# Two transformer blocks on one core: high-part weight tiles streamed as two 256-column products into one accumulator

## The reference, cut to what matters

```python
z = rms_norm(h) @ w_in                      # 2048 -> 5120, first block
h = h + mixed @ w_out                       # 2048 -> 2048
h = h + (silu(f @ ffn_w1) * (f @ ffn_w3)) @ ffn_w2     # 2048 -> 5632 -> 2048
h = h + (p @ pl_w_up) * sigmoid(h @ pl_w_gate)
...
proj = hn @ w_in_2                          # 2048 -> 12288, second block
y_a = pool(u) @ pool_w_2 ; y_b = (...) @ conv_out_w_2
h = h + (g_a * y_a + g_b * y_b) @ w_o_2
h = h + (silu(gate) * up) @ w_down_2        # 2048 -> 5632 -> 2048
```

## Time and profile before

| | |
|---|---|
| Device time, median of 3 runs | 2670.52 us (2670.02 to 2670.8) |
| Profiled execution, span from its first to its last instruction | 2668.2 us |
| Instructions in the profile | 39872, of them 15711 matmuls |
| DMA | 502.92 MB, mean 188 GB/s |

### The profile page before, as it was taken

How to read it: one execution, slowest core, us unless ns; L and a number is a source line. 1 busy time by engine, 2 the same in 40 slices (tenths; PEclk the granted TensorE clock), 3 DMA queues, 4 the chain that set the end, 5 groups by cost and what they waited for, 6 DMA issues and landing times.

```text
span 2668.2 us, 39872 instructions
## 1 busy us (share of the span) xinstructions
PE 2657.2 (100%) x15711; PEld 2349.5 (88%) x15711; DVE 1658.2 (62%) x1645; ACT 1235.8 (46%) x1355; POOL 0.8 (0%) x7
## 2 busy tenths in 40 slices
PE   9999999999999999999999999999999999999998
PEld 7889888888888888888999999888888888888887
DVE  6567766555655556796676666556765645564555
ACT  5446554444444444565443333444554434443444
POOL 0000000000000000000000000000000000000000
PEclk9999999999999999999999999999999999999999
DMA  8554555556555555555555555555565555555554
GB/s 291 183 174 144 192 187 189 191 189 191 192 191 191 191 191 188 175 197 198 176 183 178 179 184 190 189 189 189 189 205 189 189 190 189 189 195 195 178 190 140
DMA packets 254251, 502.92 MB, mean 188 GB/s; under 512 B 8130, under 2 KB 11652, under 8 KB 253988
## 3 DMA queue, kind: packets, MB, share of 16 engines
q1 hardware_dynamic: 252180, 497.61, 56.5%
q10 hardware_dynamic: 1952, 3.68, 0.4%
HBM read 498.37 MB, written 2.88 MB: 188 GB/s over the span
## 4 chain that ended last, share of the span: by engine, by line
PE 99%; DVE 0%; ACT 0%; DMA 0%; issue 0%; ACTq 0%; DVEq 0%
PE ps L1356 49%; PE ps L1370 24%; PE ps L1389 4%; PE ps L1390 4%; PE ps L1391 4%; PE ps L1407 4%; PE ps L1408 4%; PE ps L1409 4%; PE ps L1399 0%; PE ps L1401 0%; PE ps L1400 0%; PE ps L1319 0%; DMA xtok<-in_x_dram 0%; PE ps L1543 0%; PE ps L1542 0%; PE ps L1544 0%
## 5 line engine op out<-in xcount | busy, mean ns | idle before, releaser
L822 DVE TENSOR_TENSOR lo<-raw,hi 128x1024 fp32r<-128x1024 f32 x940 | 1127.6, 1223 | 856.5 <-ACT hi L488 847.6
L488 ACT ACTIVATE hi<-raw 128x1024 fp32r<-128x1024 f32 x940 | 971.3, 1055 | 1065.3 <-PE ps L1370 479.0
L1356 PE MATMUL ps<-A,hi 128*128 128x512 f32 x3648 | 859.9, 392 | 0.0
L1356 PEld LDWEIGHTS ps<-A,hi 128*128 128x128 f32 x3648 | 675.1, 188 | 138.9
L1356 PE MATMUL ps<-B,hi 128*128 128x512 f32 x1984 | 481.7, 395 | 0.0
L1370 PEld LDWEIGHTS ps<-A,lo 128*128 128x128 f32 x3648 | 442.6, 188 | 11.5 <-DVE lo L822 0.2
L1370 PE MATMUL ps<-A,lo 128*128 128x256 f32 x3648 | 445.4, 278 | 0.0
L1356 PEld LDWEIGHTS ps<-B,hi 128*128 128x128 f32 x1984 | 364.4, 188 | 79.3
L1370 PEld LDWEIGHTS ps<-B,lo 128*128 128x128 f32 x1984 | 243.0, 188 | 10.3
L1370 PE MATMUL ps<-B,lo 128*128 128x256 f32 x1984 | 244.5, 277 | 0.0
L1408 PE MATMUL ps<-B,hi 128*128 128x258 f32 (+1 forms) x768 | 219.8, 286 | 0.0
(11 more groups left out here) (240 smaller groups left out, 1341.1 us busy)
## 6 DMA issues: line engine op xcount, KB each, us to landing
raw<-in_w_in_dram SPq DMA_DIRECT2D x136, 1024.0 KB, 5.1
raw<-in_ffn_w_dram SPq DMA_DIRECT2D x132, 1024.0 KB, 5.1
raw<-in_w_gate_up_dram SPq DMA_DIRECT2D x88, 1024.0 KB, 5.0
raw<-in_w_down_dram SPq DMA_DIRECT2D x44, 1024.0 KB, 5.1
raw<-in_w_out_dram SPq DMA_DIRECT2D x16, 1024.0 KB, 5.1
raw<-in_pl_w_gate_dram SPq DMA_DIRECT2D x16, 1024.0 KB, 5.1
raw<-in_conv_out_w_dram SPq DMA_DIRECT2D x16, 1024.0 KB, 5.1
raw<-in_w_o_dram SPq DMA_DIRECT2D x16, 1024.0 KB, 5.1
```

The costliest lines, as they stand in the source:

```text
L488: act.activation(hi[:, slot % RING], raw[:, raw_slot, 2 * (slot % 2):2 * (slot % 2) + 2, :], ACT.Copy).then_inc(hi_ready, 1)
L822: dve.tensor_tensor(lo[:, slot % RING], raw[:, slot // 2 % RAWS, 2 * (slot % 2):2 * (slot % 2) + 2, :], hi[:, slot % RING], ALU.subtract). ...
L1356: last = pe.matmul(ps[:, b0 + m, :], high(slot, kk, m), both, start=j == 0 and kk == 0, stop=ends and j == seg.pieces - 1 and kk == 1)
```

## The change

Every product of a high weight tile with 512 columns becomes two products with 256 columns: four tiles with Xh, then the same four with Xl. All three kinds of product add to columns 0 to 255 of a bank. ACT's copy of the second accumulators and DVE's addition are taken out. DVE's first operation of each group now reads PSUM itself and frees the banks; for plup and plgate it is a plain copy. ACT waits for `psum_free` of the group where it waited for DVE's `asked`. Ahead of the first attention scores TensorE waits for `psum_free` of the last qk group. Matmuls in other layouts, loads and splits stay.

```diff
-            def copy_second(kind, G, end, b0):
-
-                act.wait_ge(pieces_used, end)
-                act.wait_ge(psum_free, G)
-                if SQUARED & {kind, before[0]}:
-                    wait(ready)
-                before[0] = kind
-                act.activation(pb_copy[:, :, :], ps[:, b0:b0 + 4, T:2 * T], ACT.Copy).then_inc(copied, 1)
+            def wait_group(G):
+
+
+                act.wait_ge(psum_free, G + 1)
+                act.nop(nofuse=True)
...
-            def add_halves(G, b0, to):
-                second.skip()
-                wait(second)
+            def sums_done(end):
+
+                dve.wait_ge(pieces_used, end)
                 wait(given)
                 wait(ready)
-                dve.tensor_tensor(to, ps[:, b0:b0 + 4, 0:T], pb_copy[:, :, :], ALU.add).then_inc(psum_free, 1)
+
+            def free_sums(ins, G):
+
+                ins.then_inc(psum_free, 1)
                 dve.wait_ge(psum_free, G + 1)
...
                 elif kind in ("gate", "ga", "gbr"):
-                    add_halves(G, b0, work[:, :, :])
-                    hand(dve.tensor_tensor(work[:, :, :], work[:, :, :], Rm, ALU.mult))
+                    sums_done(end)
+                    free_sums(dve.tensor_tensor(work[:, :, :], sums, Rm, ALU.mult), G)
...
                 elif kind in ("up", "cb"):
-                    add_halves(G, b0, work[:, :, :])
-                    step(dve.tensor_tensor(work[:, :, :], work[:, :, :], Rm, ALU.mult))
+                    sums_done(end)
+                    free_sums(dve.tensor_tensor(work[:, :, :], sums, Rm, ALU.mult), G)
...
                 elif kind == "plgate":
                     hk = some(h, k, 4, 0, T)
-                    add_halves(G, b0, work[:, :, :])
+                    sums_done(end)
+                    free_sums(dve.tensor_copy(work[:, :, :], sums), G)
...
                 X = activations(buf, layout)
+                at = 0 if layout == "halves" else META
                 pe.wait_ge(hi_ready, n + 1)
                 for kk in range(2):
                     k = 2 * j + kk + (4 * WIDEST_FIRST[g] if seg.name == "pool" else 0)
-                    for m in range(MT):
-                        both = X[:, k, 0:2 * T] if layout == "halves" else X[:, k, META:META + 2 * T]
-                        last = pe.matmul(ps[:, b0 + m, :], high(slot, kk, m), both, start=j == 0 and kk == 0,
-                                         stop=ends and j == seg.pieces - 1 and kk == 1)
+                    for part in range(2):
+                        x = X[:, k, at + part * T:at + (part + 1) * T]
+                        for m in range(MT):
+                            last = pe.matmul(ps[:, b0 + m, 0:T], high(slot, kk, m), x, start=j == 0 and kk == 0 and part == 0,
+                                             stop=ends and j == seg.pieces - 1 and kk == 1 and part == 1)
...
                         if hd == 0:
-                            v_in.skip(4)
                             wait(v_in)
+                            pe.wait_ge(psum_free, QK.g0 + 4)
```

More of the change, by code:

```diff
@@ L131 @@
 PER = {
[L132 to L135, removed]
+    "res_ffn": (2, 0, 2, 1), "part": (0, 0, 0, 0), "gate": (0, 0, 1, 0), "up": (0, 1, 1, 1),
+    "plgate": (5, 2, 4, 1), "ga": (0, 0, 1, 0), "gbr": (0, 0, 1, 0), "cv": (1, 0, 0, 0),
+    "cg": (5, 0, 0, 0), "cb": (0, 1, 1, 1), "cout": (0, 1, 1, 1), "res_ffn2": (3, 0, 2, 1),
+    "tpart": (0, 0, 0, 0),
 }
@@ L190, in turns_of @@
 def turns_of(eng, seg, tallies, run, lead=0):
-    per = [sum(PER.get(kind, (0,) * 5)[i] for kind in seg.kinds) for i in range(5)]
+    per = [sum(PER.get(kind, (0,) * 4)[i] for kind in seg.kinds) for i in range(4)]
     whole = seg.turns if seg.turns == 1 else min(seg.turns, max(seg.peel, lead))
@@ L388, in bass_two_blocks @@
         PLUP = next(s for s in SEGS if s.name == "plup")
+        QK = next(s for s in SEGS if s.name == "qk")
         def landed(n):
@@ L553, in evacuate @@
                     return
[L554 to L557, removed]
+                if kind in ("qk", "plup", "pool"):
+                    return
+                more()
+                if kind == "part":
                     return
                 if kind in ("res_ffn", "res_ffn2"):
-                    asked.skip()
-                    wait_alone(asked)
+                    wait(ready)
+                    wait_group(G)
                     given.mark(act.activation(pb_copy[:, :, :], some(h, k, 4, 0, T), ACT.Square))
@@ L579, in evacuate @@
                 elif kind == "plgate":
-                    act.wait_ge(psum_free, G + 1)
+                    wait(ready)
+                    wait_group(G)
                     given.mark(with_function(pb_copy[:, :, :], work[:, :, :], ACT.Sigmoid))
@@ L889, in evacuate @@
                     hk = some(h, k, 4, 0, T)
-                    add_halves(G, b0, work[:, :, :])
-                    step(dve.tensor_tensor(hk, hk, work[:, :, :], ALU.add))
+                    sums_done(end)
+                    free_sums(dve.tensor_tensor(hk, hk, sums, ALU.add), G)
                     more()
                 elif kind == "res_gate":
-                    add_halves(G, b0, work[:, :, :])
+                    hk = some(h, k, 4, 0, T)
+                    sums_done(end)
+                    free_sums(dve.tensor_tensor(hk, hk, sums, ALU.add), G)
                     if gi < MT - 1:
@@ L915, in evacuate @@
                 elif kind == "cout":
-                    add_halves(G, b0, work[:, :, :])
-                    step(dve.tensor_tensor(work[:, :, :], work[:, :, :], some(G2, k, 4, 0, T), ALU.mult))
+                    sums_done(end)
+                    free_sums(dve.tensor_tensor(work[:, :, :], sums, some(G2, k, 4, 0, T), ALU.mult), G)
                     hand(dve.tensor_tensor(work[:, :, :], work[:, :, :], some(G1, k, 4, 0, T), ALU.add))
@@ L921, in evacuate @@
                 elif kind == "plup":
-                    add_halves(G, b0, UP[:, k:k + 4, :])
+                    sums_done(end)
+                    free_sums(dve.tensor_copy(UP[:, k:k + 4, :], sums), G)
                 elif kind == "plgate":
                     hk = some(h, k, 4, 0, T)
-                    add_halves(G, b0, work[:, :, :])
+                    sums_done(end)
+                    free_sums(dve.tensor_copy(work[:, :, :], sums), G)
                     more()
@@ L965, in evacuate @@
                 elif kind == "pool":
-                    add_halves(G, b0, work[:, :, :])
+                    sums_done(end)
                     for i in range(MT):
-                        last = dve.scalar_tensor_tensor(out=G1[:, k + i, :], in0=work[:, i, :], scalar=gain("pscale", k + i),
+                        last = dve.scalar_tensor_tensor(out=G1[:, k + i, :], in0=ps[:, b0 + i, 0:T], scalar=gain("pscale", k + i),
                                                         in1=G1[:, k + i, :], op0=ALU.mult, op1=ALU.mult)
-                    step(last)
+                    free_sums(last, G)
                 elif kind in ("cv", "cg"):
@@ L1296, in last @@
                         dve.tensor_scalar(HT[:, a, c:e], HT[:, a, c:e], r, None, ALU.mult).then_inc(left_scaled, 1)
-            walk(dve, {0: own, 1: asked, 2: given, 3: ready, 4: second}, split, evacuate, side, last)
+            walk(dve, {0: own, 1: asked, 2: given, 3: ready}, split, evacuate, side, last)
         @block.tensor
```

28 lines of the change are left out of this document (11 added, 17 removed).

## The result

| | before | after |
|---|---|---|
| Median | 2670.44 us (2670.02 to 2670.8, 4 runs) | 2696.68 us (2690.86 to 2697.37, 4 runs) |
| Profiled execution, span | 2668.2 us | 2695.6 us |

The ratio is 1.0094, with a 95% interval of 1.0082 to 1.0106: slower, by 26.2 us. The forecast was 2686.4 us, with 2639 to 2714 as its range. The execution profiled is the longest of the four, 2697.37 us.

The account below looks back on a forecast made before the run. TensorE's distance between product starts was taken as the bound: 1299.4 us (A, PT) plus 675.0 (B) is 1974.4 against 1958.5, +15.9. With 2668.2 and 2.3 for the median that gave 2686.4 us, range 2639 to 2714.

Parts of the forecast that it names:

- What bounds the kernel: Whole span: TensorE's distance between product starts sets the time; its waits come to only 2.7 us.
- Copies, additions, waits at 0 us: ACT's copies, DVE's additions and the new waits: none ends or adds a wait of TensorE, 0 us.
- A at 117.7 ns a product: Segments reading A and PT: 3680 triples at the slow speed, 353.1 ns each, 1299.4 us.
- B at 113.4 ns: Segments reading B: 1984 triples at the fast speed, 340.2 ns each, 675.0 us.
- The prediction's own sign of being wrong: Profile after: wrong if the A stretch takes 174.2 us or B's 90.5, or TensorE waits at group starts.
- Rival 1: B keeps the slow speed it enters with from A, so everything is slow: +43.2, 2713.7 us; chance 0.25.
- stands once: 256-column runs in B: nearly all fast, one slow at 118.1 ns just after an entry from A.
- the forecast's own 2675 to 2697: Whole kernel: narrower range in us, allowing a sixth of B or of A at the other speed, and rounding.
- Rival 2, all fast: Entries to A's segments: an unbroken stream holds 113.4 ns in A and B; -31.6, 2638.9 us; chance 0.23.
- Weight loads: 5664 more loads with the split products: hidden, their cost inside the product distances, nothing added.
- The toll per matmul: Each split product: the skill's flat 2.5 ns per matmul, estimated +14.2 us; rows spoke against it as whole story.

Follow-up runs that it names:

- e1: The kernel before with TensorE's split into 256-column products alone, ACT's copies and DVE's additions kept: 2694.07 us, ratio 1.0094.
- e12: e11's TensorE stream built on the kernel before, with second accumulators, ACT's copies and DVE's additions kept: 2642.68 us, ratio 0.9897.
- e11: e2 with four identity transposes at the start of each turn of the first up-projection and of plgate: 2642.93 us, ratio 0.9898.
- e2: The changed kernel with two small buffers put elsewhere, so A and B's halves both begin 64 bytes past a multiple of 256: 2669.61 us.
- e4: The changed kernel with one small buffer put between A and B, both beginning 192 bytes past a multiple of 256: 2715.12 us.
- e10: e2 with four identity transposes ahead of each of the two turns of the first down-projection alone: 2650.88 us, ratio 0.9927.
- e9: e2 with four identity transposes at each turn of the first block's first up- and first down-projection: 2646.01 us, ratio 0.9908.
- e8: The kernel before, without the split, with its buffers at e2's places: 2674.52 us, ratio 1.0016.

## Why the prediction was right, and where its sum was short

- **What bounds the kernel.** Held. TensorE is the path before and after, and no wait appeared.
- **Copies, additions, waits at 0 us.** Held; shown by e1 against the change, 2694.07 and 2696.68 us with ranges that overlap, and by e12 against e11, 2642.68 and 2642.93.
- **A at 117.7 ns a product.** Held: 180.9 us for the stretch, 180.8 foretold. The row that carried it was segment u, the only stream before with 256-column products alone. It reads the same A, at the same place.
- **B at 113.4 ns.** This is the term that was mis-sized. It held for out, the cb groups, gbr, wo and most of ga, and failed for the three down-projections of the first block and the start of ga: 768 + 768 + 576 + 168 = 2280 of 5952 products at 117.8 ns, 2280 x 4.4 ns = 10.0 us. 15.9 + 10.0 = 25.9 us, against 25.5 by the two lines' shares (a tenth of a per cent is 2.7 us) and 27.4 by the span. The prediction's own sign of being wrong, a B stretch of 90.5 us where 87.1 was foretold, was met: 90.4. Rival 1 had named this step and priced it for all of B; it came true for 38% of it.
- **A row misread.** The prediction says that a slow run of Wl·Xh in B "stands once", after the entry into ga. In the same trace the first such run after the entry into each of the three down-projections is slow too, and the next one fast:

```profile
529.53 3.77 PE ps L1370 x32
540.77 3.64 PE ps L1370 x32
...
794.94 3.77 PE ps L1370 x32
806.17 3.64 PE ps L1370 x32
...
1016.25 3.77 PE ps L1370 x32
```

  After the entries into out and wo the first run is fast. So B's segments that begin slow in the kernel before, three down-projections and ga, the cb groups aside, are those that went slow in the profile after, where no 512-column products break the stream behind the entry; priced at 10.0 us they would have given 2696.4 us. That fits this profile and is not proof: three of the four cb groups begin slow before and all were fast after, and e1's profile, with the same order of products on TensorE, has the down-projections fast and out slow.
- **What was luck.** The sign. The prediction had no term for the place of the buffers, and the same instructions took 2669.61 us at e2's places, which is no change, and 2715.12 at e4's. Slower by 26 us holds for A at 192 and B at 64 alone. The median is also just inside the forecast's own 2675 to 2697, and one of the four runs was 6 us under it.
- **Rival 2, all fast.** Not met by the change, but its mechanism is real with A at 64: there a stream held at the fast speed carries it through A and B (e10), and with most of it fast the kernel takes 2642.93 us, where the bound was 2638.9. With A at 192, as in the change, a stream that came in fast from B went slow at the entry (e1).
- **Weight loads.** No cost of the 5664 more shows: the triple of 3 x 113.3 ns has three of them and is shorter than the 344.3 ns of before with two.
- **The toll per matmul.** The Trainium skill (TensorE: Matmul & The Clock Gate, Back-to-back issue gap) gives columns / 2.4 GHz plus about 2.5 ns as the gap of a matmul by itself, +14.2 us for the split as an estimate; for streams of weight load and matmul it gives about 131 ns at 512 columns, far under the 229.0 and 233.1 ns here. The runs disagree with both: with the same number of products the split cost 45 us by e4 and gained 27 by e11, the granted clock at 1.00 in every stretch shown.

What stays open: why a start falls into the one speed or the other (four transposes did both), why one side step or crossing throws the stream out and another sets it right, and what differs between executions of one program, 2690.86 to 2697.37 us here. Only two places were tried, 64 and 192, with the weights left where they were; whether it is the place itself or the distance to the weights that counts, and whether 256 bytes is the period, no run tells.

## What to carry to other kernels

Where matmuls follow each other without a wait, take the cost of a product from the distance between starts in a stream of the same shape all through, and look for more than one speed with the same instructions; a mean over runs that a different shape keeps breaking doesn't carry over. Look at the first run after each change of buffer too, and don't put a slow one aside as an exception: here four of them lay where the changed kernel was then slow. Before judging a change of shape, try it with the operands at two or three places: here that moved the same program from 2715 to 2670 us, more than the change itself. Work taken off engines that end no wait of the bound one was worth nothing here; e12 against e11 showed it with one more kernel.

## What the runs showed of the hardware that was not expected

- Two held speeds for the same 256-column float32r products, 113.3 and 117.8 ns, 6.6 and 11.1 ns over 256 columns at 2.4 GHz, each kept for over a thousand products and, where A and B lay at the same place (e2, e4, e9 to e12), across every direct change between them; where they lay at different places, that change alone could turn it (e1).
- The place of the moving rows, 192 or 64 bytes past a multiple of 256, sets the distance of 512-column products, 229.0 or 233.1 ns (the earlier trace rows and e8), and how readily 256-column streams are slow: with both buffers at 192 (e4) the time is within 1.5 us of what 5664 slow triples give.
- Four transposes of 128 columns, about half a microsecond, can change the speed of the hundreds of microseconds behind them, either way: 2669.61 us without any (e2), 2667.65, 2646.01, 2650.88 and 2642.93 us with them at different places.
